# Two-layer decoder trunk, one core: norm sums in one product, squares folded on GpSimd, last norm by token

## The reference, cut to what matters

```python
def swiglu(x, wg, wu, wd):
    return (jax.nn.silu(x @ wg) * (x @ wu)) @ wd
...
        xp = layer_norm(ALPHA * xp + yp, ln_g[layer, 0], ln_b[layer, 0])
        xp = layer_norm(ALPHA * xp + swiglu(xp, w_ffn_gate[layer], w_ffn_up[layer], w_ffn_down[layer]),
                        ln_g[layer, 1], ln_b[layer, 1])
```

## Time and profile before

| | |
|---|---|
| median of 3 runs | 3721.32 us |
| profiled execution | 3722.03 us, span 3720.2 us |
| mean granted TensorE clock | 0.939 of full |
| PE busy | 3443.2 us (93%) |
| DVE busy | 1238.5 us (33%) |
| ACT busy | 708.6 us (19%) |
| POOL busy | 1015.7 us (27%) |
| first norms | from about 1454 and 2867 us |
| second norm of layer 0 | from about 2235 us |
| last norm | from about 3650 us to the end |

### The profile page before, as it was taken

One profiled execution on the slowest core, in us unless ns is written; L12 is line 12 of the kernel. 1 busy time (PEld: TensorE's weight loads), 2 busy tenths in 40 slices (PEclk: granted clock), 3 DMA queues, 4 the chain that ended last, 5 costly groups with the idle time before them and its releaser, 6 DMA issues. The chain is left out here.

```text
span 3720.2 us, 55802 instructions
## 1 busy us (share of the span) xinstructions
PE 3443.2 (93%) x22142; PEld 3136.8 (84%) x22142; DVE 1238.5 (33%) x2450; ACT 708.6 (19%) x1426; POOL 1015.7 (27%) x546
## 2 busy tenths in 40 slices
PE   8998778998989769999999999998879999999997
PEld 7997556676766559999999998997659999999996
DVE  6713545555555432200004215113652300003123
ACT  1101333433434321200001102101230200001002
POOL 3542111101112024222223342321335122233231
PEclk9999889998999869999999999998769999999999
DMA  3112332323233570111111112110122011111111
GB/s 128 50 45 56 105 108 80 94 75 88 77 84 84 147 254 24 35 45 45 46 52 43 47 45 74 47 49 24 52 71 78 25 53 48 45 45 43 47 47 46
DMA packets 327225, 246.83 MB, mean 66 GB/s; under 512 B 28336, under 2 KB 321977, under 8 KB 325356
## 3 DMA queue, kind: packets, MB, share of 16 engines
q1 hardware_dynamic: 325668, 233.52, 21.7%
q10 hardware_dynamic: 720, 8.55, 0.6%
q0 software_dynamic: 640, 2.10, 0.2%
HBM read 219.54 MB, written 45.63 MB: 71 GB/s over the span
## 5 line engine op out<-in xcount | busy, mean ns | idle before, releaser
L556 PE MATMUL ps<-X_rounded,c_w_hi 128*128 128x344 f32 x2712 | 872.7, 322 | 10.2 <-issue 7.2
L558 PE MATMUL ps<-X_rounded,c_w_rounded 128*128 128x344 f32 x2712 | 869.5, 321 | 0.0
L557 PE MATMUL ps<-c_xla,c_w_hi 128*128 128x344 f32 x2112 | 675.5, 320 | 0.0
L556 PEld LDWEIGHTS ps<-X_rounded,c_w_hi 128*128 128x128 f32 x2712 | 510.7, 188 | 12.3 <-issue 7.7
L502 POOL CAST c_w_hi<-c_w 128x2048 fp32r<-128x2048 f32 (+2 forms) x101 | 156.5, 1550 | 1322.8 <-DMA c_w<-in_w_ffn_up 763.4
L558 PEld LDWEIGHTS ps<-X_rounded,c_w_rounded 128*128 128x128 f32 x2712 | 510.2, 188 | 0.0
L557 PEld LDWEIGHTS ps<-c_xla,c_w_hi 128*128 128x128 f32 x2112 | 399.0, 189 | 0.4
L504 POOL TENSOR_TENSOR c_w_rounded<-c_w,c_w_hi 128x2048 fp32r<-128x2048 f32 (+2 forms) x101 | 378.9, 3751 | 8.1
L556 PE MATMUL ps<-c_f_hi,c_w_hi 128*128 128x344 f32 x1056 | 343.6, 325 | 13.1 <-DVE c_f_lo L931 13.1
L558 PE MATMUL ps<-c_f_hi,c_w_rounded 128*128 128x344 f32 x1056 | 341.2, 323 | 0.0
L557 PE MATMUL ps<-c_f_lo,c_w_hi 128*128 128x344 f32 x1056 | 339.6, 322 | 0.0
(11 more groups left out here) (484 smaller groups left out, 5553.4 us busy)
## 6 DMA issues: line engine op xcount, KB each, us to landing
X<-in_cache_nsa_kv SPq DMA_DIRECT2D x256, 192.0 KB, 2.4
c_w<-in_w_ffn_gate SPq DMA_DIRECT2D x44, 512.0 KB
c_w<-in_w_ffn_up SPq DMA_DIRECT2D x44, 512.0 KB
c_w<-in_w_ffn_down SPq DMA_DIRECT2D x32, 704.0 KB, 4.7
v_packed<-in_cache_nsa_kv SPq DMA_DIRECT2D x256, 64.0 KB, 2.5
in_even_w<-in_w_in_even SPq DMA_DIRECT2D x52, 256.0 KB, 3.1
c_w<-in_w_in_odd SPq DMA_DIRECT2D x50, 256.0 KB, 3.2
x_spilled<-H ACTq DMA_DIRECT2D x2, 4128.0 KB, 12.0
```

What stands on the lines that cost most here:

```text
L556: pe.matmul(dst, whi, xhi, start=first, stop=False)
L557: pe.matmul(dst, whi, xlo, start=False, stop=False)
L558: return pe.matmul(dst, wlo, xhi, start=False, stop=last)
```

## The change

**Sums.** `collect` stays as it is for rows 0 to 5. Rows 6 and 7 are now added by VectorE (`total`), so that a mean is one product. This holds for both norms of layer 0 and the first of layer 1.

**Squares.** In the first norm of each layer GpSimd adds the 8 squared rows of a chunk in three halving steps (`fold`: 4 rows to 4, 2 to 2, 1 to 1), into `sums_a`, and the variance is one product. In the second norm of layer 0 VectorE does it for chunk 0 with one reduction; chunks 1 and 2 keep their eight products.

**Order.** `out` and `down_chunk` can be cut by rows k, and means and variances are put inside. `seq_up` becomes (0,0), (1,0), (0,1), (1,1), (0,2), (1,2). Low parts are counted row by row, and the first product of a chunk waits for one row at a time (`fresh`). In the first norm ScalarE runs the inverse root and `finish` of chunk 2 after two silus, VectorE scales and splits chunk 2 before the third `hide`.

**Weights.** In the up stage the gate and the up weights have a semaphore each, are fetched and split separately; slot 0 is refilled after the fifth gate product and the fifth up product.

**Last norm.** X is transposed before it is normed. For each tile TensorE makes 8 transposes and 8 products with X as the weights and one column of the 1/1024 matrix (`turn`), which gives the mean of each token. VectorE keeps the negated mean (`centre_row`), ScalarE squares the centred tile of 1024 elements with an accumulated sum and makes the inverse root of one column, VectorE applies mean and gain (`shape`) and inverse root and bias (`settle`) to a tile of 1024. Gain and bias lie in SBUF as rows, the same on every partition. There are four buffers.

```diff
@@ chain_phase
-    seq_up = [(0, 0), (1, 0), (0, 1), (0, 2), (1, 1), (1, 2)]
+    seq_up = [(m, c) for c in range(NB) for m in range(2)]
...
+        tile_bank = (6, 6, 3, 6, 3, 1, 6, 3, 1)
+        user = {1: 0, 3: 1, 4: 2, 6: 3, 7: 4, 8: 5}
@@ fetch_up
-                if n >= 2:
-                    sp.wait_ge(upped, {2: 4, 3: 6}.get(n, 3 * (n - 1)))
                 for part, (_, src) in enumerate(up_src(n)):
+                    if n >= 2:
+                        sp.wait_ge(upped if part else gated, {2: 5, 3: 6}.get(n, 3 * (n - 1)))
@@ GpSimd
+            def fold(c):
+                sq = na.rows[:, :, cols(c)]
+                pool.wait_ge(na.squared, c + 1)
+                pool.tensor_tensor(sq[:, 0:4], sq[:, 0:4], sq[:, 4:8], ALU.add).then_inc(na_halved, 1)
+                pool.wait_ge(na_halved, 2 * c + 1)
+                pool.tensor_tensor(sq[:, 0:2], sq[:, 0:2], sq[:, 2:4], ALU.add).then_inc(na_halved, 1)
+                pool.wait_ge(na_halved, 2 * c + 2)
+                pool.wait_ge(na.mean_ready, c + 1)
+                pool.tensor_tensor(sums_a[:, c, :], sq[:, 0], sq[:, 1], ALU.add).then_inc(na.folded, 1)
...
+            for c in range(NB):
+                fold(c)
             for n in range(2, KF):
                 split_up(n)
@@ TensorE
-            out(6, 1)
-            mean(na, 0, evicted_o, 20)
+            out(6, 1, range(4))
+            mean(na, 0)
+            out(6, 1, range(4, KD))
             out(7, 1)
-            out(6, 2)
+            out(6, 2, range(5))
             variance(na, 0)
-            mean(na, 1, evicted_o, 22)
+            out(6, 2, range(5, KD))
+            mean(na, 1)
             out(7, 2)
...
             for s, (m, c) in enumerate(seq_up):
-                pe.wait_ge(na.low_ready, c + 1)
...
-                up(m, m, c, s % 3 * 2, 0)
+                up(m, m, c, s % 3 * 2, 0, m == 0)
                 if s == 1:
+                    variance(na, 1)
...
+                up(m, m, c, s % 3 * 2, 1)
                 if s == 0:
-                    mean(na, 2, evicted_o, 24)
-                    variance(na, 1)
+                    mean(na, 2)
-                if s == 1:
+                if s == 2:
                     variance(na, 2)
...
+            def turn(n):
+                rows = tiles[n][1]
+                pe.wait_ge(evicted_d, (44, 44, 46, 46, 46, 48, 48, 48, 48)[n])
+                if n in user:
+                    pe.wait_ge(row_shaped, user[n] + 1)
+                for k in range(KD):
+                    mm = pe.transpose(r.ps[0:rows, tile_bank[n] + k // 4, k % 4 * P:(k % 4 + 1) * P],
+                                      r.X[:, k, n * P:n * P + rows], r.ident[:])
+                mm.then_inc(turned, 1)
+                if n:
+                    pe.wait_ge(row_centred, n)
+                for k in range(KD):
+                    mm = pe.matmul(r.ps[0:rows, 0, n:n + 1], r.X[:, k, n * P:n * P + rows], r.ones_d[:, 0:1],
+                                   start=(k == 0), stop=(k == KD - 1))
+                mm.then_inc(row_mean, 1)
...
+            if odd:
+                down_chunk(14, 1, range(4))
+                mean(nb, 0)
+                down_chunk(14, 1, range(4, KH))
+                down_chunk(15, 1)
+                variance(nb, 0)
+                down_chunk(14, 2, range(4))
+                mean(nb, 1)
+                down_chunk(14, 2, range(4, KH))
+                down_chunk(15, 2)
+                variance(nb, 1)
+                mean(nb, 2)
+            else:
+                down_chunk(14, 1)
+                turn(0)
+                down_chunk(15, 1)
+                turn(1)
+                down_chunk(14, 2, range(4))
+                turn(2)
+                down_chunk(14, 2, range(4, KH))
+                turn(3)
+                turn(4)
+                down_chunk(15, 2)
+                for n in range(5, 9):
+                    turn(n)
@@ ScalarE, first norm
-            norm(na)
-            for s in range(6):
+            square(na, 0)
+            inverse_root(na, 0)
+            finish(na, 0)
+            square(na, 1)
+            inverse_root(na, 1)
+            square(na, 2)
+            finish(na, 1)
+            for s in range(2):
+                light(s, s % 3 * 2)
+            act.preload_act_table_set("natural_log_exp_and_others")
+            inverse_root(na, 2)
+            finish(na, 2)
+            for s in range(2, 6):
@@ ScalarE, last norm, for each tile
+                    act.activation(junk[0:rows, :], got, ACT.Square, bias=row_stat[0:rows, n, 0:1],
+                                   accum_out=row_stat[0:rows, n, 1:2]).then_inc(row_squared, 1)
...
+                    act.activation(row_stat[0:rows, n, 2:3], row_stat[0:rows, n, 1:2], ACT.Ln, bias=r.bias[0:rows, 0:1],
+                                   scale=1 / D).then_inc(row_logged, 1)
...
+                    act.activation(row_stat[0:rows, n, 2:3], row_stat[0:rows, n, 2:3], ACT.Exp,
+                                   scale=-0.5).then_inc(row_rstd, 1)
@@ VectorE
+            def total(nm, c, m, evicted, need, n):
...
+                v.tensor_tensor(sums[:, c, :], sums[:, c, :], r.X[:, m, cols(c)], ALU.add).then_inc(nm.totalled, 1)
+            def fold(nm, c):
+                v.wait_ge(nm.squared, c + 1)
+                v.tensor_reduce(sums_b[:, c, :], nm.rows[:, :, cols(c)].rearrange("p k n -> p n k"), AX.X,
+                                ALU.add).then_inc(nm.folded, 1)
...
             add_out(18, 6, 0)
+            total(na, 0, 6, evicted_o, 19, 0)
             add_out(19, 7, 0)
+            total(na, 0, 7, evicted_o, 20, 1)
             add_out(20, 6, 1)
             centre(na, 0)
+            total(na, 1, 6, evicted_o, 21, 2)
             add_out(21, 7, 1)
+            total(na, 1, 7, evicted_o, 22, 3)
             add_out(22, 6, 2)
+            total(na, 2, 6, evicted_o, 23, 4)
             scale(na, 0)
             low(na, 0)
+            centre(na, 1)
             add_out(23, 7, 2)
-            centre(na, 1)
+            total(na, 2, 7, evicted_o, 24, 5)
             centre(na, 2)
             scale(na, 1)
             low(na, 1)
-            scale(na, 2)
-            low(na, 2)
...
             for s, (m, c) in enumerate(seq_up):
+                if s == 2:
+                    scale(na, 2)
+                    low(na, 2)
@@ VectorE, second norm of layer 0
+                add_down(42, 14, 0)
+                total(nb, 0, 6, evicted_d, 43, 0)
+                add_down(43, 15, 0)
+                total(nb, 0, 7, evicted_d, 44, 1)
+                centre(nb, 0)
+                add_down(44, 14, 1)
+                total(nb, 1, 6, evicted_d, 45, 2)
+                fold(nb, 0)
+                add_down(45, 15, 1)
+                total(nb, 1, 7, evicted_d, 46, 3)
+                scale(nb, 0)
+                centre(nb, 1)
+                add_down(46, 14, 2)
+                total(nb, 2, 6, evicted_d, 47, 4)
+                low(nb, 0)
+                add_down(47, 15, 2)
+                total(nb, 2, 7, evicted_d, 48, 5)
+                centre(nb, 2)
@@ VectorE, last norm
+                def shape(n):
...
+                    v.scalar_tensor_tensor(out=stage[0:rows, n % 4, :], in0=got, scalar=row_stat[0:rows, n, 0:1],
+                                           in1=g_row[0:rows, :], op0=ALU.add, op1=ALU.mult).then_inc(row_shaped, 1)
+                def settle(n):
...
+                    v.scalar_tensor_tensor(out=stage[0:rows, n % 4, :], in0=stage[0:rows, n % 4, :],
+                                           scalar=row_stat[0:rows, n, 2:3], in1=b_row[0:rows, :], op0=ALU.mult,
+                                           op1=ALU.add).then_inc(row_settled, 1)
...
+                add_down(47, 15, 2)
+                centre_row(5)
+                for n in range(5, 9):
+                    if n < 8:
+                        centre_row(n + 1)
+                    shape(n)
+                    settle(n)
```

More of the change, by code:

```diff
@@ L423, in chain_phase @@
         w_in_o = [nc.alloc_semaphore(f"{tag}_w_in_o{u}") for u in range(3)]
-        w_in_u = [nc.alloc_semaphore(f"{tag}_w_in_u{u}") for u in range(2)]
+        w_in_u = [[nc.alloc_semaphore(f"{tag}_w_in_u{u}_{part}") for part in range(2)] for u in range(2)]
         w_in_d = [nc.alloc_semaphore(f"{tag}_w_in_d{u}") for u in range(3)]
@@ L715, in _ @@
                         pe.wait_ge(w_split_p, 4)
[L716 to L719 removed]
+                    project(m, m + 1, c, m == 0)
                     if n == 1:
@@ new lines, in _ @@
+                add_down(43, 15, 0)
+                add_down(44, 14, 1)
+                centre_row(0)
+                shape(0)
+                settle(0)
+                add_down(45, 15, 1)
+                centre_row(1)
+                shape(1)
+                settle(1)
+                centre_row(2)
+                shape(2)
+                settle(2)
+                add_down(46, 14, 2)
+                centre_row(3)
+                shape(3)
+                centre_row(4)
```

(5 more changed lines are left out.)

252 lines of the change are left out of this document (113 added, 139 removed).

## The result

The changed kernel takes 3697.36 us (median of 6 runs, 3687.16 to 3705.24), the kernel before beside it 3716.73 us (6 runs, 3709.27 to 3721.37). The ratio is 0.9947, 95% interval 0.9924 to 0.9970: 19.7 us less, between 11 and 28. Profiled execution against profiled execution it is 3722.03 to 3705.24 us, 16.8 less. Measured again with the experiments (`c1_as_changed`) the ratio was 0.9962 (0.9949 to 0.9975), 14 us less. The forecast was 3705 us and 16.3 us less. One execution of e1_all_products took 13302 us for no known reason and is left out of its ratio; no other lies more than 0.4% from the median of its kernel.

A forecast was written before the change was run, and what follows sets the result against it. TensorE, busy 93% of the span, was taken as the bound. First norms 0, second norm −3.7 and last norm −12.6 sum to −16.3 us, from 3722.03 profiled to 3705.7, or 3705 as median; range 3684 to 3718.

The forecast's parts named there:

- First norms: 0 forecast (0.6 and −0.5): First norm of each layer: removed work against added stalls and clock, 0.6 us gained in layer 0, 0.5 lost in layer 1.
- the walk: Row-by-row timing of the changed first norm: added stalls 17.4 us in layer 0, reaching the mark 4.5 us earlier.
- Rival C: First norms: halvings run well above the slope, deciding from a fold of 8.6 us; at double, 3740 us; chance 0.06.
- The fourth wait: First norm, layer 0: TensorE waits 7.5 us for chunk 1's low parts, VectorE 5.7 us late from turn-taking with GpSimd's fold.
- the two long stalls also halve the clock, 1.9 each: First norms: slow restarts behind the two long stalls, 1.9 us each, 3.8 us in layer 0.
- rival D: Every added first-norm stall brings a clock fall, four a layer, and the second norm gives nothing: 3716 us; chance 0.07.
- the prediction's size for it: VectorE's reduction of chunk 0 in the second norm put at 3.0 us, from L861's 3.02 us for 2752 elements.
- The weights: hidden: Up stage: refetching slot 0 later, a half needs 8.2 us against 11.3 us until use, so costs nothing.
- Second norm: 3.7 forecast: Second norm of layer 0: 10.9 us earlier, less 5.3 us and one clock fall of 1.9; ends 10.9 and 0.
- the collision: Second norm: first low parts take turns with GpSimd's two weight splits, costing 5.3 us and a clock fall of 1.9.
- Last norm: 12.6 forecast: Last norm: tiles of 2.65 us at full clock, 5.3 at half, gain 12.6 us; ends 20.4 gained and 1.3 lost.
- Rival B: Last norm: half clock from tile 0 on, down products slowed too, gain 3 instead of 12.6 us: 3715 us; chance 0.15.

The follow-up runs named there:

- c1_as_changed: The changed kernel unaltered, run again as reference on the chip of the next three experiments: 3695.57 us, ratio to before 0.9962.
- e1_all_products: Against the changed kernel, GpSimd's folds in both first norms removed, each variance eight products again: 3687.56 us, ratio to before 0.9936.
- e3: Against the changed kernel, first norms' folds made by VectorE, one reduction per chunk, instead of GpSimd's halvings: 3677.11 us, ratio to before 0.9911.
- e8: Changed kernel with GpSimd's second and third weight splits held back in the second norm of layer 0: 3698.81 us, ratio to before 0.9964.
- e6: Changed kernel with the second norm's chunk 0 variance by eight products instead of VectorE's reduction: 3696.38 us, ratio to before 0.9969.
- e4: Changed kernel with the last norm's rows added by GpSimd and VectorE, one mean product per tile instead of eight: 3682.87 us, ratio to before 0.9924.
- e2: Changed kernel with only chunk 2's fold removed in both first norms, its variance eight products: 3689.19 us, ratio to before 0.9942.
- e7: Changed kernel with e3 and e4 together, chunk 0 of first norms by products, VectorE's last addition moved earlier: 3666.55 us, ratio to before 0.9877.
- e9: e7 with e8's held-back splits added: 3662.42 us (4 runs), ratio to before 0.9858.

## Why the prediction was right

**First norms: 0 forecast (0.6 and −0.5), 0.3 and −0.9 measured.** In the first execution each wait stood where the walk had put it: 5.9 forecast and 5.78 measured, 1.2 and 1.26, 2.8 and 2.62. The fold, 3.1 + 1.7 + 0.9 with two hand-overs of 0.08, was 3.08 + 1.63 + 0.91. Rival C, which needed a fold of 8.6 us, fell with that. The fourth wait was mis-sized: 7.5 forecast, 4.72 in layer 0 and 6.17 in layer 1. VectorE was late nearly as forecast (8.25 for scalings instead of 3.99, 4.63 for low parts instead of 3.98, 4.9 in all for 5.7), but TensorE was late too. The step that failed is "the two long stalls also halve the clock, 1.9 each": the stall of 2.62 us halved it as well, and 24 passes took 6.67 us instead of 4.2. So layer 0 has three falls for two, the late low parts found TensorE late as well, and waits and clock come to 14.4 + 6.2 us where 17.4 + 3.8 were put down (6.2: product and passes behind each wait took 3.7, 7.4 and 9.7 us, and take 2.2, 4.6 and 7.8 at full clock). The two errors nearly cancel; of what is left, 0.9 us in layer 0, the place isn't known. A fixed price of 1.9 us per long stall is itself wrong: behind the same wait of 5.78 us it was 1.5 in the first execution and 2.7 in layer 0 of c1, behind the same 2.62 us it was 2.8 and 1.3 in the two layers of the first and nothing in layer 0 of c1. The stretch hardly feels this (85.7 and 85.3 us), since a fall also fills time that would have been waited. For the same reason rival D, whose falls behind the shorter stalls came in part, had the price wrong.

**The reduction.** The Trainium skill's "GPSIMD Engine Reference", section "4.1 Engine selection", gives sums along the free dimension to VectorE. The runs agree in what is better: e3 is 13 us under the changed kernel in the first norms. They do not bear out the prediction's size for it, 3.0 us from L861; the rows show

```profile
2240.06 5.36 DVE L914 TENSOR_REDUCE c_sums_b<-c_yb 128x344 f32<-128x2752 f32 x1 [1.23 <-ACT c_yb L809]
```

in the second norm and 5.06 to 5.53 us in the first. TensorE's waits for chunks 0 and 1 shrink by only 0.7 and 0.5 us with it; most of its gain is that VectorE doesn't take turns with itself.

**The weights: hidden, as forecast.** TensorE waits for no half of them in the up stage; a half's load took 3.9 us at the median.

**Second norm: 3.7 forecast, 6.7 in one execution and 1.7 in the other.** Two steps are in it. The reduction was to be ready 11.1 us after the stretch's first row, just as TensorE asks. It was ready after 13.4 us, the 2.4 us by which 5.36 is more than 3.0, and cost a wait where none was put down, and a slow restart of 1.6 us behind it in six of ten executions:

```profile
2245.47 0.56 PE L595 MATMUL ps<-c_sums_b,ones_d 128*128 128x344 f32 x1 [2.55 <-DVE c_sums_b L914]
```

And the collision was taken to hold TensorE up every time, by 5.3 and 1.9 us. It does not: of the eight executions with the reduction and without e8's edit six have 59.5 to 60.5 us and two 64.4 and 64.5 (e6, without the reduction, 65.2). Where it holds TensorE up, as in c1, TensorE waits 3.61 us, and the 48 passes behind it take 10.3 us instead of 7.8, 6.1 us together. Which of the two comes is set by that restart (c1_as_changed above), a coupling that the walk did not have. The gain over the eight is 5.3 us on the mean; the forecast of 3.7 lies between the two outcomes and meets neither.

**Last norm: 12.6 forecast, 13.9 measured.** The tile was put at 2.65 us at full clock and is 2.7 (1.04 and 1.84, overlapping by 0.15), at half 5.0 to 5.2. VectorE's two passes are 1.28 each, 1.3 forecast. Tile 5 ran at full clock, 7 and 8 at half, 6 began at full: as put down, but for half of tile 6. Tiles 3 and 4 on end cost 2.7 us of clock over the next down product and 0.45 in tile 4 itself, forecast 1.9; in e3's execution they cost none. Rival B fell: tiles 0 to 2, with 1.9 to 5.2 us of full products between them, kept 1.00.

The Trainium skill's "TensorE: Matmul & The Clock Gate", section "LDWEIGHTS (loading the stationary operand)", gives P / 1.2 ns for P columns, which is 107 ns for 128, and names no clock. Sixteen records of L728 take 1.84 us at full clock, 0.115 each, which agrees, and 3.41 at half, 0.213 each, which does not. Had the page's figure held at both, the tiles 6 and 7 would have taken 2.7 us.

**What remains.** The sum of the four stretches, 20.0 and 15.2 us, explains the measured 19.7 and 14.1 within their intervals. That the first profiled execution came out 16.8 us lower, half a microsecond from the forecast, is partly luck: the four stretches gave 3.7 us more than forecast, 3.0 of it in the second norm, the stages between them took 2.1 us back, and the rest is time outside the span. What moves the stages between them, by up to 8 us in the one before the first norm of layer 1, is open.

## What to carry to other kernels

Before work is moved off the bounding engine, ask who waits for it: here a fold of 5.9 us replaced 4.05 us of products three times in a chain that had no slack, and lost, while the same idea in the last norm, one sum product per tile made while other products run, gained 15 us. Two engines that are both off the path can still meet on it: VectorE's and GpSimd's two-operand work in SBUF takes turns, so give a sum to whichever of them is running already, or hold one back. Price a wait on TensorE with the slow restart behind it as a range, read from more than one execution, and ask what that restart shifts, here the fetches and so the splits. Compare stretches from the same row to the same row when stages elsewhere vary by more than the edit is worth.

## What was not expected of the hardware

A VectorE reduction of 344 sums of eight elements, 344 columns of each of eight rows, takes 5.06 to 5.53 us for 2752 elements, where a subtraction of as many takes 3.02: 1.95 against 1.10 ns an element.

Tiles with eight one-column products let the granted clock fall although TensorE is busy all the time (5.00 of 5.00 us at 0.50), and tiles 5 to 7 of e4, 24 transposes and three such products in 3.3 us, did not (1.00).

The length of a wait does not settle what the clock does behind it. In the norms of the kernels after, waits up to 1.3 us cost no clock. Of three waits of 1.98 us (e1, e2) one cost 1.5 us, of six of 2.1 us (e3, e7, e9) four did (the 24 passes behind them took 5.38 to 5.75 us, and 4.20 or 4.21 behind the other two), of sixteen of 2.6 to 2.7 us in first norms eleven cost 1.3 to 2.8 us and five nothing, among them 2.62 us in layer 0 of c1 and 2.72 in layer 1 of e9. The waits of 3.6 us and more all cost clock, 1.4 to 3.4 us each.
